# Latent attention: features of queries and keys on the partitions, both latents scaled once, the non-rotary transposes gone

## The chip, the cores and the metric

The kernel runs on one core of one Trainium2 chip. The metric is the device time of one execution, in microseconds. The kernel before took 1671.33 us (median of 3 runs, 1671.21 to 1671.62).

## The reference, cut to what matters

One block of a hybrid encoder, 256 tokens, model width 2048: latent attention with 16 heads, a convolution branch, gates, an attention over a memory, a SwiGLU. The change is in the latent attention alone:

```python
q = (rms_norm(c_q, norm_cq) @ w_uq).reshape(B, S, MLA_HEADS, QK_NOPE + QK_ROPE)      # 512 -> 16 x (128 + 64)
q = jnp.concatenate([q[..., :QK_NOPE], apply_rope(q[..., QK_NOPE:], cos, sin)], axis=-1)
kv = (rms_norm(c_kv, norm_ckv) @ w_ukv).reshape(B, S, MLA_HEADS, QK_NOPE + V_HEAD)   # 256 -> 16 x (128 + 128)
k_nope, v = kv[..., :QK_NOPE], kv[..., QK_NOPE:]
k_r = apply_rope(k_rope[:, :, None, :], cos, sin)                                    # one rotary key for all heads
```

The scores of a head are the product of its query and key over 128 non-rotary and 64 rotary features; a softmax with a chunk-causal mask and the product with v follow.

## The kernel before, in words

All weights stream through a ring of four tiles (128 x 1024 f32 at most). SP issues one DMA a tile into `raw`; ACT rounds the tile to fp32r (`split_hi`, L776 to L782, tile `w_hi`), DVE makes the remainder (`split_lo`, L1254 to L1260, tile `w_lo`), and TensorE (PE) multiplies three times per block of 128 input features: lo by hi, hi by lo, hi by hi (`products`, L349 to L369, the matmuls on L364 to L366). Here the activations are the stationary operand (128 features x 128 tokens) and the weights the moving one (512 columns), so the product comes out with tokens on the partitions, in `acc`, two PSUM banks, one for each half of the tokens. `tile_done` gives a ring slot back to ACT and `acc_free[b]` a bank to PE.

The order is written by hand, for each engine. The parts that the change touches:

- **Projection (L431 to L472).** Tiles 0 to 7 make c_q (512 columns), tiles 8 to 15 c_kv and the rotary key (320 columns); four chunks of eight tiles for the convolution follow. ACT copies c_q and later c_kv to `stage` and sums its squares; POOL makes the row factors 1/rms (`row_factor`, L1849). PE turns c_q's `stage` behind the second of the tiles 8 to 15 (`pos == 1`, L460), c_kv's behind the second tile of the next chunk (L467), the turned rotary key behind the fourth (L470). ACT and DVE turn these into `cqT` and `ckvT` with the gains of the norms (L865, L906, L1327, L1373). The factors 1/rms are not applied yet.
- **Eight pairs of heads (`gate_and_pair`, L528 for PE, L956 for ACT, L1450 for DVE).** A pair is eight gate tiles, two tiles of w_uq (`tile_products`, L564 to L581: 384 moving columns, 24 matmuls), two half-wide tiles of w_ukv (`kv_products`, L548 to L562: 512 columns, 12 matmuls). ACT copies the queries to `q_tok` and keys and values to `kv_tok`, tokens on the partitions, and applies 1/rms there (L970 to L984). POOL turns the rotary queries by their angles (`query_rope`, L1893) into `qr_tok`.
- **Attention of a pair, spread over the gate tiles of the next one (`attention`, L475 for PE, L925 for ACT).** Behind gate tile 1 PE transposes q_tok (4 blocks), kv_tok (4) and qr_tok (2), and ACT copies them to `qnT`, `knT`, `qrT` (features on the partitions). Behind tile 3 come the scores, behind tile 6 the transposes of the probabilities, behind tile 7 the product with the values.

Of the kernel before, what the change touches and what calls it, by code (L numbers as in the profile page):

```python
# [24 lines left out]
ALU = mybir.AluOpType  # L25
# [66 lines left out]
def program(nc, x, memT, positions, vecs, w_in, w_uq, w_ukv, w_dwT, w_pw2, b_pw2, w_o, w_q_mem, w_kv_mem,  # L92
# [10 lines left out]
    with ctx:  # L103
# [54 lines left out]
        q_tok = sb(early, "q_tok", [P, NB, 2, NOPE + ROPE])  # L158
        kv_tok = sb(early, "kv_tok", [P, NB, 2, NOPE + VH])
# [72 lines left out]
        qr_turned, qr_out = sem("qr_turned"), sem("qr_out")  # L232
# [112 lines left out]
        def _(pe):  # L345
# [95 lines left out]
            for t in range(8, 16):  # L441
# [18 lines left out]
                if pos == 1:  # L460
                    turn_stage(Q_CQ, 2 * (S_A + 1))


            for c in range(4):
                for t in range(8):
                    products(T_B + 8 * c, t, 8, mixT, 2 * t, 2, CH, C_B + c)
                    if t == 1 and c == 0:  # L467
                        pe.wait_ge(stage_full, 2 * (S_A + 2))
                        turn_group(Q_CKV, 0, [stage[:, b, k * P:(k + 1) * P] for k in range(2) for b in range(NB)])
                    if t == 3 and c == 0:  # L470
                        pe.wait_ge(kr_ready, 1)
                        turn_group(Q_CKV, 1, [qr_tok[:, b, :, :].rearrange("p h d -> p (h d)") for b in range(NB)])  # L472


            def attention(t, p, q):  # L475

                if t == 0:
                    pe.wait_ge(q_ready, 2 * p + 2)
                    turn_group(q, 0, [q_tok[:, b, h, 0:NOPE] for h in range(2) for b in range(NB)])
                    pe.wait_ge(kv_ready, 2 * p + 2)  # L480
                    turn_group(q, 1, [kv_tok[:, b, h, 0:NOPE] for h in range(2) for b in range(NB)])
                if t == 1:
                    pe.wait_ge(rope_ready, p + 1)
                    if not (isinstance(p, int) and p == 0):
                        pe.wait_ge(qr_out, p)
                    for b in range(NB):
                        ins = turn(xt[:, b * P:(b + 1) * P], qr_tok[:, b, :, :].rearrange("p h d -> p (h d)"),
                                   ident[:, :])
                    ins.then_inc(qr_turned, 1)
                if t == 2:  # L490
                    operand_ready(q)
                    pe.wait_ge(qr_out, p + 1)
# [22 lines left out]
                if t == 7:  # L515
# [3 lines left out]
                    for h in range(2):  # L519
                        mm(ov[:, h * VH:(h + 1) * VH], probsT[:, h, 0:P], kv_tok[:, 0, h, NOPE:],  # L520
                           start=True, stop=True)
                        for kb in range(2):
                            ins = mm(ov[:, (2 + h) * VH:(3 + h) * VH], probsT[:, h, (1 + kb) * P:(2 + kb) * P],  # L523
                                     kv_tok[:, kb, h, NOPE:], start=kb == 0, stop=kb == 1)
# [3 lines left out]
            def gate_and_pair(i, first, last=False):  # L528
# [15 lines left out]
                for t in range(2):  # L544
                    tile_products(i * 12 + T_C, 8 + t, t, 2, cqT, 2 * t, 2, UQ, i * 3 + (C_C + 1))
                kv_products(i * 12 + T_C, i * 3 + (C_C + 2))

            def kv_products(base, chunk):  # L548

                pe.wait_ge(lo_done, base + 12)  # L550
                for b in range(NB):
                    pe.wait_ge(acc_free[b], chunk)
                    for k in range(2):
                        hi, lo = (ckvT[j][:, k, b * P:(b + 1) * P] for j in range(2))
                        whi, wlo = w_hi[:, (10 + k) % RING, 0:CH], w_lo[:, (10 + k) % RING, 0:CH]
                        mm(acc[:, b, :], lo, whi, start=k == 0, stop=False)  # L556
                        mm(acc[:, b, :], hi, wlo, start=False, stop=False)
                        ins = mm(acc[:, b, :], hi, whi, start=False, stop=k == 1)
                        if b == 1:
                            ins.then_inc(tile_done, 1)  # L560
                    if b == 0:
                        ins.then_inc(acc0_full, 1)  # L562

            def tile_products(base, t, pos, n_tiles, lhs, k0, kt, n, chunk):  # L564

                s = t % RING
                first, last = pos == 0, pos == n_tiles - 1
                pe.wait_ge(lo_done, base + (t + 1))
                for b in range(NB):
                    if first:  # L570
                        pe.wait_ge(acc_free[b], chunk)
                    for k in range(kt):
                        hi = lhs[0][:, k0 + k, b * P:(b + 1) * P]
                        lo = lhs[1][:, k0 + k, b * P:(b + 1) * P]
                        o = acc[:, b, 0:n]
                        mm(o, lo, w_hi[:, s, k * n:(k + 1) * n], start=first and k == 0, stop=False)  # L576
                        mm(o, hi, w_lo[:, s, k * n:(k + 1) * n], start=False, stop=False)  # L577
                        ins = mm(o, hi, w_hi[:, s, k * n:(k + 1) * n], start=False, stop=last and k == kt - 1)  # L578
                    if last and b == 0:
                        ins.then_inc(acc0_full, 1)  # L580
# [192 lines left out]
        def _(act):  # L773
# [85 lines left out]
            for t in range(8):  # L859
# [5 lines left out]
                if t == 2:  # L865
# [25 lines left out]
            for c in range(4):  # L891
                for t in range(8):
# [13 lines left out]
                    if c == 0 and t == 2:  # L906
                        turned_hi_part(0, 2 * Q_CKV + 1, [ckvT[0][:, k, :] for k in range(2)],
                                       gain=[vcol("norm_ckv", k) for k in range(2)])
                    if c == 0 and t == 4:
# [15 lines left out]
            def attention(t, p, q):  # L925
                if t == 0:
                    act.wait_ge(turned, 2 * q + 1)
# [5 lines left out]
                if t == 1:  # L933
                    act.wait_ge(qr_turned, p + 1)
                    fn(qrT[:, :], xt[:, 0:TOK], ACT.Copy).then_inc(qr_out, 1)
# [20 lines left out]
            def gate_and_pair(i, first, last=False):  # L956
                for t in range(12):
# [7 lines left out]
                    if t == 9:  # L965

                        if not first:
                            act.wait_ge(turned, 2 * i + (2 * Q_C - 1))
                            act.wait_ge(rope_ready, i)
                        for b in range(NB):  # L970
# [1006 lines left out]
```

## Time and profile before

| | |
|---|---|
| median of 3 runs | 1671.33 us |
| the profiled execution's own time | 1671.39 us |
| its span in the trace | 1669.6 us |
| around the span | 1.8 us |
| PE (matmul) busy | 1653.5 us, 99% |
| PEld (weight load) busy | 1375.3 us, 82% |
| DVE / ACT / POOL busy | 1127.3 / 827.7 / 102.2 us |

A row of the timeline gives the start of an instruction (or of several alike, merged, with their count), its duration and its engine. The matmuls are pipelined and the ends in their rows are modelled: a matmul's duration is longer than the time until the next one starts. What a matmul costs is read from start to start.

### The profile page before, as it was taken

The page shows a single profiled execution, that of the slowest core. Times are in us where ns is not written, and L with a number is a line of the kernel's source. Part 1 is how long each engine was busy: PE and PEld are TensorE (multiplying, and loading weights), DVE is VectorE, ACT ScalarE, POOL GpSimd, SP SyncE. Part 2 cuts the span into 40 slices and gives each one's busy share as a digit, 9 for nine tenths or more (in the row PEclk, how much of TensorE's full clock was granted, in tenths as well). Part 3 has the DMA queues.
Part 4 walks back from the last instruction along what each step waited for, and adds up shares of the span by engine and source line. Part 5 has one row for each costly group of instructions (what it writes and reads, how often), then busy time and mean ns, then how long its engine had stood idle before and what let it go on. Part 6 is the DMA issues. An engine that isn't in the chain of part 4 may idle for free.

```text
span 1669.6 us, 23695 instructions
## 1 busy us (share of the span) xinstructions
PE 1653.5 (99%) x7696; PEld 1375.3 (82%) x7696; DVE 1127.3 (68%) x1461; ACT 827.7 (50%) x1057; POOL 102.2 (6%) x152
## 2 busy tenths in 40 slices
PE   9999999999999999999999999999999999999997
PEld 7888888888888888878888788888888888888886
DVE  5578777778986457886559856666666666654453
ACT  7556555556546444566545644444444444444343
POOL 3100100011000000120001200000000000000000
PEclk9999999999999999999999999999999999999999
DMA  7865555555675665554445666666666666565563
GB/s 228 248 208 163 168 165 154 166 157 165 182 212 181 192 212 182 182 190 158 144 139 187 190 191 198 191 191 196 184 187 198 201 191 198 191 219 184 182 213 134
DMA packets 161106, 309.68 MB, mean 185 GB/s; under 512 B 10240, under 2 KB 16896, under 8 KB 160800
## 3 DMA queue, kind: packets, MB, share of 16 engines
q1 hardware_dynamic: 158864, 301.50, 58.8%
q0 software_dynamic: 1488, 6.42, 1.0%
q10 hardware_dynamic: 704, 1.11, 0.2%
q8 instruction: 29, 0.48, 0.1%
q14 instruction: 21, 0.17, 0.0%
HBM read 306.89 MB, written 2.10 MB: 185 GB/s over the span
## 4 chain that ended last, share of the span: by engine, by line
PE 91%; DVE 4%; issue 2%; ACT 1%; DMA 0%; SPq 0%; DVEq 0%; ACTq 0%; POOLq 0%; POOL 0%
PE acc L364 28%; PE acc L366 27%; PE acc L365 27%; DVE w_lo L1259 2%; PE tp L376 1%; DVE x_f L1598 1%; PE acc L576 1%; PE acc L578 1%; PE acc L577 1%; PE sc L499 1%; DMA raw<-in_w_in_dram 0%; PE ov L523 0%; ACT w_hi L782 0%; PE sc L504 0%; PE acc L556 0%
## 5 line engine op out<-in xcount | busy, mean ns | idle before, releaser
L1259 DVE TENSOR_TENSOR w_lo<-raw,w_hi 128x1024 fp32r<-128x1024 f32 (+3 forms) x591 | 718.0, 1220 | 432.4 <-ACT w_hi L782 422.4
L782 ACT ACTIVATE w_hi<-raw 128x1024 fp32r<-128x1024 f32 (+3 forms) x591 | 605.5, 1027 | 758.6 <-PE acc L366 726.1
L364 PE MATMUL acc<-w_hi,crossT 128*128 128x512 f32 x832 | 324.8, 390 | 0.8 <-DVEq L1616 0.8
L366 PE MATMUL acc<-w_hi,crossT 128*128 128x512 f32 x832 | 323.9, 389 | 0.0
L365 PE MATMUL acc<-w_lo,crossT 128*128 128x512 f32 x832 | 323.8, 389 | 0.0
L364 PE MATMUL acc<-w_hi,mixT 128*128 128x512 f32 x732 | 290.0, 396 | 1.8 <-ACTq L877 0.5
L366 PE MATMUL acc<-w_hi,mixT 128*128 128x512 f32 x732 | 285.6, 390 | 0.0
L365 PE MATMUL acc<-w_lo,mixT 128*128 128x512 f32 x732 | 285.0, 389 | 0.0
L364 PEld LDWEIGHTS acc<-w_hi,crossT 128*128 128x128 f32 x832 | 156.2, 188 | 33.9 <-issue 1.5
L366 PEld LDWEIGHTS acc<-w_hi,crossT 128*128 128x128 f32 x832 | 156.2, 188 | 32.5
L365 PEld LDWEIGHTS acc<-w_lo,crossT 128*128 128x128 f32 x832 | 156.2, 188 | 32.1
L364 PEld LDWEIGHTS acc<-w_hi,mixT 128*128 128x128 f32 x732 | 137.4, 188 | 35.2 <-issue 4.8
L366 PEld LDWEIGHTS acc<-w_hi,mixT 128*128 128x128 f32 x732 | 137.4, 188 | 29.5
L365 PEld LDWEIGHTS acc<-w_lo,mixT 128*128 128x128 f32 x732 | 137.6, 188 | 27.2
L1391 DVE SCALAR_TENSOR_TENSOR conv<-uT,wdwT,conv (+1 forms) x240 | 118.2, 493 | 19.5 <-DVE conv L1391 16.7
L366 PE MATMUL acc<-w_hi,actT 128*128 128x512 f32 x336 | 130.7, 389 | 0.0
L365 PE MATMUL acc<-w_lo,actT 128*128 128x512 f32 x336 | 130.7, 389 | 0.0
L364 PE MATMUL acc<-w_hi,actT 128*128 128x512 f32 x336 | 130.7, 389 | 0.0
L1725 DVE STREAM_TRANSPOSE row_bc<-stage 32x256 f32<-32x256 f32 x176 | 76.7, 436 | 3.6
L364 PEld LDWEIGHTS acc<-w_hi,actT 128*128 128x128 f32 x336 | 63.1, 188 | 13.2
L366 PEld LDWEIGHTS acc<-w_hi,actT 128*128 128x128 f32 x336 | 63.1, 188 | 13.2
L365 PEld LDWEIGHTS acc<-w_lo,actT 128*128 128x128 f32 x336 | 63.1, 188 | 12.8
(264 smaller groups left out, 1527.0 us busy)
## 6 DMA issues: line engine op xcount, KB each, us to landing
raw<-in_w_in_dram SPq DMA_DIRECT2D x104, 512.0 KB, 3.8
raw<-in_w_gate_dram SPq DMA_DIRECT2D x88, 512.0 KB, 4.3
raw<-in_w_up_dram SPq DMA_DIRECT2D x88, 512.0 KB, 3.8
raw<-in_w_down_dram SPq DMA_DIRECT2D x80, 512.0 KB, 4.0
raw<-in_w_kv_mem_dram SPq DMA_DIRECT2D x64, 512.0 KB, 3.9
raw<-in_w_o_dram SPq DMA_DIRECT2D x32, 512.0 KB, 4.4
raw<-in_w_q_mem_dram SPq DMA_DIRECT2D x32, 512.0 KB, 3.7
raw<-in_w_o_mem_dram SPq DMA_DIRECT2D x32, 512.0 KB, 3.7
```

What stands on the lines that cost most here:

```text
L364: mm(o, lo, whi, start=first and k == 0, stop=False)
L365: mm(o, hi, wlo, start=False, stop=False)
L366: ins = mm(o, hi, whi, start=False, stop=end)
L376: ins = turn(tp[:, bank, j * P:(j + 1) * P], src, ident[:, :])
L499: mm(sc[:, h, at:at + keys], qnT[:, h, qs:qs + P], knT[:, h, 0:keys], start=qs == 0, stop=False, skip_group_check=True)
L576: mm(o, lo, w_hi[:, s, k * n:(k + 1) * n], start=first and k == 0, stop=False)
L577: mm(o, hi, w_lo[:, s, k * n:(k + 1) * n], start=False, stop=False)
L578: ins = mm(o, hi, w_hi[:, s, k * n:(k + 1) * n], start=False, stop=last and k == kt - 1)
L782: fn(w_hi[:, s, 0:width], raw[:, s, 0:width], ACT.Copy).then_inc(hi_done, 1)
L1259: V.tensor_tensor(w_lo[:, s, 0:width], raw[:, s, 0:width], w_hi[:, s, 0:width].bitcast(F32), ALU.subtract).then_inc(lo_done, 1)
L1391: ins = V.scalar_tensor_tensor(out=a, in0=u, scalar=wt, in1=a, op0=ALU.mult, op1=ALU.add)
L1725: ins = V.transpose(dst[:, :, :, 32 * i:32 * i + 32], src[:, :, :, 32 * j:32 * j + 32])
```

## The change

The non-rotary queries and the keys are made with the weights stationary (128 input features x 128 output features) and the turned latent moving (256 tokens), so they come out of `acc` with the features on the partitions, and ACT copies them straight to `qnT` and `knT`. The rotary queries and the values are still made with tokens on the partitions, now 128 and 256 moving columns. Since a row factor can't be applied to a token that lies on the columns, POOL scales both latents in `stage` before they are turned, and the turns move to later tiles. Only the rotary queries are still transposed, each half through a bank of `tp`.

In the diff, in the order of the file: PE's projection, attention, `kv_products` and `q_products` (which takes the place of `tile_products`), ACT, DVE, POOL.

```diff
-                if pos == 1:
+                if pos == 5:
+                    pe.wait_ge(cq_scaled, 2)
                     turn_stage(Q_CQ, 2 * (S_A + 1))
...
-                    if t == 1 and c == 0:
-                        pe.wait_ge(stage_full, 2 * (S_A + 2))
+                    if t == 4 and c == 0:
+                        pe.wait_ge(ckv_scaled, 2)
                         turn_group(Q_CKV, 0, [stage[:, b, k * P:(k + 1) * P] for k in range(2) for b in range(NB)])
-                    if t == 3 and c == 0:
                         pe.wait_ge(kr_ready, 1)
                         turn_group(Q_CKV, 1, [qr_tok[:, b, :, :].rearrange("p h d -> p (h d)") for b in range(NB)])
...
-                if t == 0:
-                    pe.wait_ge(q_ready, 2 * p + 2)
-                    turn_group(q, 0, [q_tok[:, b, h, 0:NOPE] for h in range(2) for b in range(NB)])
-                    pe.wait_ge(kv_ready, 2 * p + 2)
-                    turn_group(q, 1, [kv_tok[:, b, h, 0:NOPE] for h in range(2) for b in range(NB)])
...
-                        ins = turn(xt[:, b * P:(b + 1) * P], qr_tok[:, b, :, :].rearrange("p h d -> p (h d)"),
-                                   ident[:, :])
-                    ins.then_inc(qr_turned, 1)
+                        turn_group(q, b, [qr_tok[:, b, :, :].rearrange("p h d -> p (h d)")])
...
+                    pe.wait_ge(q_ready, 2 * p + 2)
+                    pe.wait_ge(kv_ready, 2 * p + 2)
...
             def kv_products(base, chunk):
 
                 pe.wait_ge(lo_done, base + 12)
+                pe.wait_ge(acc_free[0], chunk)
+                for h in range(2):
+                    o = acc[:, 0, h * TOK:(h + 1) * TOK]
+                    at = slice(h * (NOPE + VH), h * (NOPE + VH) + NOPE)
+                    for k in range(2):
+                        hi, lo = (ckvT[j][:, k, :] for j in range(2))
+                        whi, wlo = w_hi[:, (10 + k) % RING, at], w_lo[:, (10 + k) % RING, at]
+                        mm(o, whi, lo, start=k == 0, stop=False)
+                        mm(o, wlo, hi, start=False, stop=False)
+                        ins = mm(o, whi, hi, start=False, stop=k == 1)
+                ins.then_inc(acc0_full, 1)
+                pe.wait_ge(acc_free[1], chunk)
                 for b in range(NB):
-                    pe.wait_ge(acc_free[b], chunk)
+                    o = acc[:, 1, b * 2 * VH:(b + 1) * 2 * VH]
                     for k in range(2):
                         hi, lo = (ckvT[j][:, k, b * P:(b + 1) * P] for j in range(2))
-                        whi, wlo = w_hi[:, (10 + k) % RING, 0:CH], w_lo[:, (10 + k) % RING, 0:CH]
-                        mm(acc[:, b, :], lo, whi, start=k == 0, stop=False)
-                        mm(acc[:, b, :], hi, wlo, start=False, stop=False)
-                        ins = mm(acc[:, b, :], hi, whi, start=False, stop=k == 1)
+                        whi, wlo = (w[:, (10 + k) % RING, 0:CH].rearrange("p (h d) -> p h d", h=2)[:, :, NOPE:]
...
+            def q_products(base, pos, chunk):
+
+                s = (8 + pos) % RING
+                first, last = pos == 0, pos == 1
+                pe.wait_ge(lo_done, base + (9 + pos))
+                if first:
+                    pe.wait_ge(acc_free[0], chunk)
+                wv = [w[:, s, 0:2 * UQ].rearrange("p (k h d) -> p k h d", k=2, h=2) for w in (w_hi, w_lo)]
+                for h in range(2):
+                    o = acc[:, 0, h * TOK:(h + 1) * TOK]
+                    for k in range(2):
+                        hi, lo = (cqT[j][:, 2 * pos + k, :] for j in range(2))
+                        whi, wlo = (w[:, k, h, 0:NOPE] for w in wv)
+                        mm(o, whi, lo, start=first and h == 0 and k == 0, stop=False, skip_group_check=True)
+                        mm(o, wlo, hi, start=False, stop=False, skip_group_check=True)
+                        ins = mm(o, whi, hi, start=False, stop=last and k == 1, skip_group_check=True)
+                if last:
+                    ins.then_inc(acc0_full, 1)
+                if first:
+                    pe.wait_ge(acc_free[1], chunk)
                 for b in range(NB):
-                    if first:
-                        pe.wait_ge(acc_free[b], chunk)
-                    for k in range(kt):
-                        hi = lhs[0][:, k0 + k, b * P:(b + 1) * P]
-                        lo = lhs[1][:, k0 + k, b * P:(b + 1) * P]
-                        o = acc[:, b, 0:n]
-                        mm(o, lo, w_hi[:, s, k * n:(k + 1) * n], start=first and k == 0, stop=False)
-                        mm(o, hi, w_lo[:, s, k * n:(k + 1) * n], start=False, stop=False)
-                        ins = mm(o, hi, w_hi[:, s, k * n:(k + 1) * n], start=False, stop=last and k == kt - 1)
-                    if last and b == 0:
-                        ins.then_inc(acc0_full, 1)
+                    o = acc[:, 1, b * 2 * ROPE:(b + 1) * 2 * ROPE]
+                    for k in range(2):
+                        hi, lo = (cqT[j][:, 2 * pos + k, b * P:(b + 1) * P] for j in range(2))
+                        whi, wlo = (w[:, k, :, NOPE:] for w in wv)
+                        mm(o, lo, whi, start=first and b == 0 and k == 0, stop=False, skip_group_check=True)
+                        mm(o, hi, wlo, start=False, stop=False, skip_group_check=True)
+                        ins = mm(o, hi, whi, start=False, stop=last and k == 1, skip_group_check=True)
                 ins.then_inc(tile_done, 1)
...
-                if t == 2:
+                if t == 6:
...
-                    if c == 0 and t == 2:
+                    if c == 0 and t == 5:
...
-                    if c == 0 and t == 4:
+                    if c == 0 and t == 5:
...
                         act.wait_ge(scores_ready, 2 * p)
-                    fn(qnT[:, :, :].rearrange("p h t -> p (h t)"), tp[:, 0, :], ACT.Copy).then_inc(turned_out[0], 1)
-                    act.wait_ge(turned, 2 * q + 2)
-                    fn(knT[:, :, :].rearrange("p h t -> p (h t)"), tp[:, 1, :], ACT.Copy).then_inc(turned_out[1], 1)
...
-                    fn(qrT[:, :], xt[:, 0:TOK], ACT.Copy).then_inc(qr_out, 1)
+                    for b in range(NB):
+                        fn(qrT[:, b * P:(b + 1) * P], tp[:, b, 0:P], ACT.Copy).then_inc(turned_out[b], 1)
...
+                            act.wait_ge(scores_ready, 2 * i)
...
-                        for b in range(NB):
+                        for b, (dst, width) in enumerate(((qnT[:, :, :].rearrange("p h t -> p (h t)"), CH),
+                                                          (q_tok[:, :, :, :].rearrange("p b h d -> p (b h d)"), TOK))):
                             acc_full(b, i * 3 + (C_C + 1), i * 12 + (T_C + 10))
-                            fn(q_tok[:, b, :, :].rearrange("p h d -> p (h d)"), acc[:, b, 0:UQ], ACT.Copy,
-                               scale=rfac[:, R_CQ, b:b + 1]).then_inc(q_ready, 1)
+                            fn(dst, acc[:, b, 0:width], ACT.Copy).then_inc(q_ready, 1)
                             act.wait_ge(q_ready, 2 * i + (b + 1))
                             act.sem_inc(acc_free[b], 1)
                     if t == 10:
                         if not first:
                             act.wait_ge(pv_done, i)
-                        for b in range(NB):
+                        for b, dst in enumerate((knT[:, :, :].rearrange("p h t -> p (h t)"),
+                                                 v_tok[:, :, :, :].rearrange("p b h d -> p (b h d)"))):
                             acc_full(b, i * 3 + (C_C + 2), i * 12 + (T_C + 12))
-                            fn(kv_tok[:, b, :, :].rearrange("p h d -> p (h d)"), acc[:, b, :], ACT.Copy,
-                               scale=rfac[:, R_CKV, b:b + 1]).then_inc(kv_ready, 1)
+                            fn(dst, acc[:, b, :], ACT.Copy).then_inc(kv_ready, 1)
                             act.wait_ge(kv_ready, 2 * i + (b + 1))
                             act.sem_inc(acc_free[b], 1)
...
-                if t == 10:
+                if t == 14:
...
-                    if c == 0 and t == 2:
+                    if c == 0 and t == 5:
...
             row_factor(R_CQ)
+            gp.wait_ge(r_ready, R_CQ + 1)
+            for b in range(NB):
+                G.tensor_scalar(stage[:, b, :], stage[:, b, :], rfac[:, R_CQ, b:b + 1], None, ALU.mult)\
+                    .then_inc(cq_scaled, 1)
...
             row_factor(R_CKV)
+            gp.wait_ge(r_ready, R_CKV + 1)
+            for b in range(NB):
+                G.tensor_scalar(stage[:, b, 0:KV_LORA], stage[:, b, 0:KV_LORA], rfac[:, R_CKV, b:b + 1], None,
+                                ALU.mult).then_inc(ckv_scaled, 1)
```

ACT's and DVE's parts of `cqT` and `ckvT` move with the turns (ACT from t == 2 to 6 and from 2 to 5, DVE from 10 to 14 and from 2 to 5); ACT's copy of the rotary key moves from t == 4 to 5.

## Rows read from the trace of the kernel before

**Rows 1.** The page: busy shares, granted clock, the chain by engine.

```profile
PE 1653.5 (99%) x7696; PEld 1375.3 (82%) x7696; DVE 1127.3 (68%) x1461; ACT 827.7 (50%) x1057; POOL 102.2 (6%) x152
...
PEclk9999999999999999999999999999999999999999
...
PE 91%; DVE 4%; issue 2%; ACT 1%; DMA 0%; SPq 0%; DVEq 0%; ACTq 0%; POOLq 0%; POOL 0%
```

**Rows 2.** Timeline of PE, the w_uq and w_ukv tiles of one pair.

```profile
196.08 0.61 PE L523 MATMUL ov<-kv_tok,probsT 128*128 128x128 f32 x4
196.44 0.42 PE L576 MATMUL acc<-w_hi,cqT 128*128 128x384 f32 x1
196.70 0.33 PE L577 MATMUL acc<-w_lo,cqT 128*128 128x384 f32 x1
...
200.54 0.34 PE L578 MATMUL acc<-w_hi,cqT 128*128 128x384 f32 x1
200.72 0.40 PE L556 MATMUL acc<-w_hi,ckvT 128*128 128x512 f32 x1
...
203.24 0.39 PE L558 MATMUL acc<-w_hi,ckvT 128*128 128x512 f32 x1
203.46 0.45 PE L364 MATMUL acc<-w_hi,mixT 128*128 128x512 f32 x1
203.75 0.40 PE L365 MATMUL acc<-w_lo,mixT 128*128 128x512 f32 x1
```

**Rows 3.** Timeline of PE, the transposes of one pair.

```profile
208.99 0.60 PE L376 MATMUL tp<-ident,q_tok 128*128 128x128 f32 x4
209.42 0.60 PE L376 MATMUL tp<-ident,kv_tok 128*128 128x128 f32 x4
209.86 0.38 PE L487 MATMUL xt<-ident,qr_tok 128*128 128x128 f32 x2
210.00 0.48 PE L364 MATMUL acc<-w_hi,mixT 128*128 128x512 f32 x1
```

**Rows 4.** Timeline of PE, 24 fp32r matmuls of 256 columns in the memory attention, twice.

```profile
767.29 0.28 PE L674 MATMUL sc<-row_r,memqT 128*128 128x256 f32 x1
...
770.12 0.40 PE L364 MATMUL acc<-w_hi,crossT 128*128 128x512 f32 x1
...
783.03 0.28 PE L697 MATMUL xt<-probs_mT,val_h 128*128 128x256 f32 x1
...
784.47 0.40 PE L364 MATMUL acc<-w_hi,crossT 128*128 128x512 f32 x1
```

**Rows 5.** Timeline of PE and its weight loads, two f32 products of one column.

```profile
155.99 0.64 PEld L537 LDWEIGHTS xt<-ones,sqT 128*128 128x128 f32 x4
156.22 0.50 PE L537 MATMUL xt<-ones,sqT 128*128 128x1 f32 x4
...
156.55 0.19 PEld L364 LDWEIGHTS acc<-w_hi,mixT 128*128 128x128 f32 x1
156.58 0.49 PE L364 MATMUL acc<-w_hi,mixT 128*128 128x512 f32 x1
```

**Rows 6.** Groups by line: ACT's copies out of acc and of the turned tiles.

```profile
L981 ACT ACTIVATE kv_tok<-acc,rfac 128x512 f32<-128x512 f32 x16 | 10.9, 681 | 2.5 <-PE acc L558 2.4
...
L972 ACT ACTIVATE q_tok<-acc,rfac 128x384 f32<-128x384 f32 x16 | 9.3, 583 | 3.6 <-PE acc L578 3.6
...
L935 ACT ACTIVATE qrT<-xt 128x256 f32<-128x256 f32 x8 | 3.1, 386 | 0.0
```

**Rows 7.** Timeline of POOL: the row factors of c_q and c_kv.

```profile
38.60 0.74 POOL L1851 TENSOR_TENSOR rfac<-mean_sq,minus_half 128x2 f32<-128x2 f32 x1 [9.04 <-DVE mean_sq L1294]
...
55.96 0.71 POOL L1851 TENSOR_TENSOR rfac<-mean_sq,minus_half 128x2 f32<-128x2 f32 x1 [1.95 <-DVE mean_sq L1294]
```

**Rows 8.** Groups by line: POOL's nearest operations to the scaling.

```profile
L1918 POOL COPY xs<-stage 128x1024 f32<-128x1024 f32 x2 | 2.1, 1037 | 202.7 <-DVE stage L1613 202.7
...
L1836 POOL TENSOR_SCALAR resid<-resid 128x128 f32<-128x128 f32 x1 | 1.2, 1207 | 0.1
```

**Rows 9.** Timeline of PE, projection: the turn of c_q, seventh tile of the eight, turn of the key.

```profile
38.34 1.03 PE L376 MATMUL tp<-ident,stage 128*128 128x128 f32 x8
39.14 0.39 PE L454 MATMUL acc<-w_hi,mixT 128*128 128x320 f32 x1
...
46.25 0.31 PE L454 MATMUL acc<-w_hi,mixT 128*128 128x320 f32 x1
...
61.86 0.38 PE L376 MATMUL tp<-ident,qr_tok 128*128 128x128 f32 x2
```

More of the change, by code:

```diff
@@ L157, in program @@
         ckvT = [sb(early, f"ckvT{j}", [P, 2, TOK], F32R) for j in range(2)]
-        q_tok = sb(early, "q_tok", [P, NB, 2, NOPE + ROPE])
-        kv_tok = sb(early, "kv_tok", [P, NB, 2, NOPE + VH])
+        q_tok = sb(early, "q_tok", [P, NB, 2, ROPE])
+        v_tok = sb(early, "v_tok", [P, NB, 2, VH])
+        spare = sb(early, "spare", [P, NB, 2, 2 * NOPE])
         qr_tok = sb(early, "qr_tok", [P, NB, 2, ROPE])
@@ L231, in program @@
         rope_step, rope_ready = sem("rope_step"), sem("rope_ready")
-        qr_turned, qr_out = sem("qr_turned"), sem("qr_out")
+        ckv_scaled = sem("ckv_scaled")
+        cq_scaled = sem("cq_scaled")
         scores_ready, scores_read = sem("scores_ready"), sem("scores_read")
@@ L519, in attention @@
                     for h in range(2):
-                        mm(ov[:, h * VH:(h + 1) * VH], probsT[:, h, 0:P], kv_tok[:, 0, h, NOPE:],
+                        mm(ov[:, h * VH:(h + 1) * VH], probsT[:, h, 0:P], v_tok[:, 0, h, :],
                            start=True, stop=True)
@@ L523, in attention @@
                             ins = mm(ov[:, (2 + h) * VH:(3 + h) * VH], probsT[:, h, (1 + kb) * P:(2 + kb) * P],
-                                     kv_tok[:, kb, h, NOPE:], start=kb == 0, stop=kb == 1)
+                                     v_tok[:, kb, h, :], start=kb == 0, stop=kb == 1)
                     ins.then_inc(pv_done, 1)
@@ L544, in gate_and_pair @@
                 for t in range(2):
[L545 removed]
+                    q_products(i * 12 + T_C, t, i * 3 + (C_C + 1))
                 kv_products(i * 12 + T_C, i * 3 + (C_C + 2))
@@ L551, in kv_products @@
+                ins.then_inc(acc0_full, 1)
+                pe.wait_ge(acc_free[1], chunk)
                 for b in range(NB):
-                    pe.wait_ge(acc_free[b], chunk)
+                    o = acc[:, 1, b * 2 * VH:(b + 1) * 2 * VH]
                     for k in range(2):
                         hi, lo = (ckvT[j][:, k, b * P:(b + 1) * P] for j in range(2))
-                        whi, wlo = w_hi[:, (10 + k) % RING, 0:CH], w_lo[:, (10 + k) % RING, 0:CH]
-                        mm(acc[:, b, :], lo, whi, start=k == 0, stop=False)
-                        mm(acc[:, b, :], hi, wlo, start=False, stop=False)
-                        ins = mm(acc[:, b, :], hi, whi, start=False, stop=k == 1)
+                        whi, wlo = (w[:, (10 + k) % RING, 0:CH].rearrange("p (h d) -> p h d", h=2)[:, :, NOPE:]
+                                    for w in (w_hi, w_lo))
+                        mm(o, lo, whi, start=k == 0, stop=False)
+                        mm(o, hi, wlo, start=False, stop=False)
+                        ins = mm(o, hi, whi, start=False, stop=k == 1)
@@ L1895, in query_rope @@
                 if not first:
-                    gp.wait_ge(qr_turned, p)
-                q = [q_tok[:, :, :, NOPE + 32 * k:NOPE + 32 * k + 32] for k in range(2)]
+                    gp.wait_ge(turned, 2 * p + 2 * Q_C)
+                q = [q_tok[:, :, :, 32 * k:32 * k + 32] for k in range(2)]
                 rope(q, [qr_tok[:, :, :, 32 * k:32 * k + 32] for k in range(2)], 2, rope_step, p, None)\
```

16 lines of the change are left out of this document (2 added, 14 removed).

## The prediction

> **What bounds the kernel now.** First the page: PE is busy for 99% of the span, its granted clock is in the top tenth in all 40 slices (the 2.4 GHz level), and the chain that ended last runs through PE for 91% [rows 1]. DVE and ACT have a third and a half of the span free. So a change pays by what it takes off PE's queue or puts on it; work on ACT, DVE or POOL counts only where PE waits for it. Second, the timeline of PE within a pair: it shows what each shape costs from start to start, since the durations of pipelined matmuls overlap. The pair's attention comes eight times, and in none of its stretches is PE idle before the parts that change.
>
> **What PE pays now, per pair.** The 24 matmuls of 384 columns and the 12 of 512 run from 196.44 to 203.46, 7.02 us [rows 2]. In them are 0.09 us of lead behind the f32 products (the first step is 0.26 us, the later ones 0.17: (200.72 - 196.70) / 23 = 0.175), and the 12 take (203.46 - 200.72) / 12 = 0.228 each. The first matmul behind them needs 0.29 us to its next where 0.23 is usual: 0.06 us, which I take for the wait on the bank that ACT empties. The eight transposes of q_tok and kv_tok take 209.86 - 208.99 = 0.87 us, 0.109 each [rows 3]. Together 7.02 + 0.06 + 0.87 = 7.95 us.
>
> **What takes its place.** Counted in columns nothing is saved: 24 x 384 + 12 x 512 = 15,360 before, and 48 x 256 + 24 x 128 = 15,360 after. But 36 matmuls become 72, each with a weight load of 128 x 128. So the price of a narrow matmul decides.
> - 256 columns, fp32r (24 for the queries' non-rotary part, 12 for the keys, 12 for the values): (770.12 - 767.29) / 24 = 0.118 us in one place and (784.47 - 783.03) / 12 = 0.120 in the other [rows 4]. I take 0.119: 48 x 0.119 = 5.71 us.
> - 128 columns, fp32r (24, the rotary queries): no row shows one. Below: the straight line through the wider ones, (0.228 - 0.119) / 256 columns = 0.00043 us a column, gives 0.119 - 128 x 0.00043 = 0.065. Above: a matmul of 256 columns, 0.119, if width stops to matter; and further off, what an f32 product of 128 columns costs, two recorded matmuls each: four records of L523 start at 196.08, and the next block really starts at 196.44 + 0.09, so 0.11 a record and 0.22 a product [rows 2]. Nearest is the load: the four matmuls of ONE column each (two f32 products, two records each) still take from 156.22 to 156.58, and behind the first of the loads, which is ahead of its matmul, they follow at 0.11 us up to the next at 156.55 [rows 5]. The moving work there is nearly nothing, so 0.11 us is what a weight load of this shape costs when it follows another. Transposes of 128 columns give 0.109 again [rows 3]. I take 0.110: 24 x 0.110 = 2.64 us.
>
> The Trainium skill ("TensorE: Matmul & The Clock Gate", the part on LDWEIGHTS) prices a load by its columns over 1.2 GHz, 107 ns for 128; by that rule, the rows at one column agree. The same page (the part on the issue gap) gives about 81 ns for a sustained matmul of 128 columns, and 131 ns for one of 512; no row here bears out the latter, the same shape takes 0.228 us. The sum by 81 ns is a rival below.
>
> So PE pays 0.09 + 5.71 + 2.64 = 8.44 us a pair if no wait remains: 0.49 us more than 7.95. Eight pairs: +3.9 us. The two transposes of the rotary queries stay and cost the same.
>
> **Waits inside the pair.** The keys' first matmul waits for bank 0, which ACT copies to qnT while PE runs the 12 narrow matmuls of the same tile: 12 x 0.110 = 1.32 us, plus 0.12 for the last wide one, 1.44 us from the last wide start. ACT needs 0.28 us until that matmul ends [rows 4], about 0.14 to start, 0.68 for a 512-wide copy [rows 6], and about 0.12 for its own wait and release: 1.22 us. Hidden, with 0.2 us to spare. If a narrow matmul took under 0.09 us it would not be. Bank 1 (256 wide, 0.39 us by the 256-wide copy in [rows 6], before 0.58) has 12 x 0.119 = 1.43 us, hidden. The next gate chunk waits for knT's bank for as long again, and ACT is now free sooner, so I count the 0.06 us as gone; at worst it stays, +0.5 us in all. ACT loses two 512-wide copies a pair behind gate tile 1; nothing queued behind them is late, so that is worth nothing. The scores wait for two 128-wide copies in place of three wider ones, two gate tiles (5.4 us) earlier: hidden. ACT's qnT now waits for the scores of the pair before, behind gate tile 3, over 10 us earlier: no wait. POOL's rotary work is unchanged, and PE transposes its result some 8 us behind the queries: hidden. The ring slots of the query tiles come back when half of the block is done, as before; those of the two key tiles some 0.3 us later at most, and their next tile is needed two tiles (5.5 us) on.
>
> **The projection.** POOL scales c_q after 38.60 + 0.74 = 39.34 us [rows 7], in two operations of 128 x 512. Its price isn't in the trace. From below: half of a copy of 128 x 1024, 0.52 us; from above: four times the two-step operation on 128 x 128, 4.8 us [rows 8]. PE needs it behind the sixth tile: 46.25 less the 0.80 + 0.08 us of the turn that no longer comes ahead of it [rows 9], 45.4 us. At 0.52 to 2.9 us each it is hidden. c_kv: from 56.67 us on [rows 7], two of 128 x 256, 0.26 to 2.4 us each, so by 61.5 at the latest, and PE asks for it behind the next tile after the old turn of the key, 61.86 - 0.5 + 2.73 = 64.1 us [rows 9]. Hidden. Queued behind the scaling on POOL are the first memory load, needed some 80 us later, and the key's rotation, which waits for c_kv anyway. ACT's and DVE's latent parts move by four and three tiles, and the pairs that use them begin some 90 us later. I count all of this at nothing; if the upper bounds held it would cost what rival 3 says.
>
> **Sum.** The profiled execution took 1671.39 us (its span and 1.8 us around it), 0.06 over the median. 1671.4 + 3.9 = 1675.3 us, +0.23%. About 0.2% (3.3 us) is what a measurement of this kernel can tell from no change, so this lies just beyond it. With both ends of the two prices (0.118 and the 0.1075 of q_tok's four transposes in [rows 3]; 0.120 and 0.119) a pair costs 0.38 to 0.76 us more, +3.0 to +6.1 us; with the 0.06 us kept, up to +6.5.
>
> **The rivals.**
> 1. *Loads don't gate: the price follows the columns, 0.065 us for 128.* Then 24 cost 1.56 us. For: fp32r at 256, 384 and 512 columns lies on one line, with no sign of a floor. Against: the one-column rows. But now bank 0 is late: PE would be at the keys 0.12 + 0.78 = 0.90 us behind the last wide start, ACT at 1.22: 0.32 us of new wait. 0.09 + 5.71 + 1.56 + 0.32 = 7.68, 0.27 less a pair, -2.2 us: 1669.2. Without the wait -4.7 us, 1666.7. This is the side that isn't slower; it decides below about 0.090 us a narrow matmul, where the sum breaks even. Chance 0.13, half of it beyond 0.2%.
> 2. *A narrow fp32r matmul runs at f32's price, 0.22 us.* Nothing narrower than 256 fp32r columns runs in the trace, so a lower rate there can't be excluded; against it, the weight loads of both types last the same 0.19 us. 24 x (0.22 - 0.11) = 2.64 us a pair more: 3.9 + 21.1 = +25.0 us, 1696.4. Chance 0.09.
> 3. *POOL late.* At 4.8 us an operation c_q is scaled at 49.1 us, PE stands from 45.4: +3.7 us, once, on top of the sum: 1679.0. It decides from 2.9 us an operation. Chance 0.03.
> 4. *A stretch of narrow fp32r matmuls hides part of each load.* Midway between the column line and the load, at 0.0875 us, it is 24 x 0.0875 = 2.10 and 0.05 us of wait at bank 0: nothing gained or lost, 1671.4. Chance 0.04. The 81 ns of the Trainium skill's page named above would be near this case (an estimate: 0.7 us faster than now).
>
> That the change doesn't do what it says I leave out: the diff takes out the eight transposes and doubles the matmuls, and both will be counted. A fall of the clock to 1.2 GHz in the narrow stretches has nothing for it: the transposes and one-column products leave the granted clock in the top tenth.
>
> **How the numbers follow.** The forecast's chance is 0.71; its own range is 1674.4 to 1677.9, 0.52 above 0.2% and 0.19 within. Slower: 0.52 + 0.09 + 0.03 = 0.64. Within: 0.19 + 0.07 + 0.04 = 0.30. Faster: 0.06. The range 1669.0 to 1678.0 holds the forecast, rival 4 and the better part of rival 1.
>
> **What would show it.** After: 24 matmuls of 128 columns with starts 0.11 us apart, 48 of 256 at 0.12; 8.4 us from the first query matmul to the next gate tile; no idle time of PE at the keys' first matmul; a period of the pairs 0.5 us longer than now; POOL done with c_q by 45 us, PE not idle ahead of the turn. I am wrong if the narrow matmuls stand 0.07 or 0.2 us apart, or if PE waits at a bank or in the projection.

## The result and the profile after

The changed kernel takes 1677.45 us (median of 7 runs, 1676.62 to 1678.84) against 1671.49 us before: 5.96 us more, a ratio of 1.0036 with a 95% interval of 1.0027 to 1.0045. Slower was forecast, with 1675.3 us as the likeliest time and 1678.0 as the upper end. The direction and the main mechanism held; about a third of the loss came from a place that the prediction had put down at nothing. The profiled execution is the slowest of the seven (1678.84 us), 7.4 us longer than the profiled one of the kernel before, so its rows show more of that loss than the median has.

The page of the changed kernel, to be held against [rows 1]:

```profile
PE 1660.0 (99%) x7920; PEld 1387.6 (83%) x7920; DVE 1126.1 (67%) x1461; ACT 818.0 (49%) x1049; POOL 105.8 (6%) x156
...
PE 92%; DVE 4%; issue 2%; ACT 1%; DMA 0%; DVEq 0%; POOL 0%; ACTq 0%; POOLq 0%; SPq 0%
```

PE has 224 matmuls more: 8 x 36 added, 8 x 8 transposes gone. Its timeline within a pair, the queries first (the first is a wide product behind the f32 ones, and 12 wide, 12 narrow, 12 wide, 12 narrow follow one another; then keys and values):

```profile
200.36 0.36 PE L582 MATMUL acc<-cqT,w_hi 128*128 128x256 f32 x1
...
201.88 0.22 PE L594 MATMUL acc<-w_hi,cqT 128*128 128x128 f32 x1
201.94 0.28 PE L595 MATMUL acc<-w_lo,cqT 128*128 128x128 f32 x1
...
203.06 0.28 PE L596 MATMUL acc<-w_hi,cqT 128*128 128x128 f32 x1
...
205.84 0.28 PE L596 MATMUL acc<-w_hi,cqT 128*128 128x128 f32 x1
205.95 0.33 PE L552 MATMUL acc<-ckvT,w_hi 128*128 128x256 f32 x1
206.12 0.28 PE L553 MATMUL acc<-ckvT,w_lo 128*128 128x256 f32 x1
...
208.76 0.28 PE L565 MATMUL acc<-w_hi,ckvT 128*128 128x256 f32 x1
208.88 0.40 PE L366 MATMUL acc<-w_hi,mixT 128*128 128x512 f32 x1
209.11 0.40 PE L367 MATMUL acc<-w_lo,mixT 128*128 128x512 f32 x1
```

Here a wide matmul is one of 256 moving columns and a narrow one of 128. From start to start a wide one takes (208.76 - 206.12) / 22 = 0.120 us, a narrow one (203.06 - 201.94) / 10 = 0.112. The whole stretch is 208.88 - 200.36 = 8.52 us where 8.44 was forecast and 7.02 + 0.06 + 0.87 = 7.95 stood before [rows 2, 3]: +0.57. The gate matmul behind it has its usual 0.23 us to the next: the 0.06 us of wait has gone, as forecast. The starts of the scores in the chain of waits (`sc`, eight matmuls a pair) give the period of the pairs, of the changed kernel:

```profile
185.28 1.31 PE sc L493 x8
220.22 1.31 PE sc L493 x8
...
394.81 1.31 PE sc L493 x8
430.31 1.31 PE sc L493 x8
```

and of the kernel before:

```profile
181.36 1.31 PE sc L499 x8
215.71 1.31 PE sc L499 x8
...
387.56 1.31 PE sc L499 x8
422.88 1.31 PE sc L499 x8
```

The eight starts have seven steps between them. Six take 34.91 to 34.94 us in place of 34.34 to 34.42, on average 34.92 in place of 34.37: +0.56. The last grows by 0.18 only (35.50 against 35.32). There, ACT also rounds the memory's operands, and before the change PE stood 0.58 us behind the values for the bank; now it is 0.21. With the first pair, which lies ahead of the first scores, the pairs cost about 7 x 0.56 + 0.18 = 4.1 us. But the first scores already start 3.92 us late, of which one pair's share explains 0.56. The other 3.36 us are in the projection, in this execution; of the median's 5.96 us, 5.96 - 4.1 = 1.9 are. The rows of POOL, ACT and PE there, which answer to [rows 7, 9], and between them the landing of one weight tile from the chain of waits (in brackets: idle time before, and who ended it):

```profile
38.50 0.74 POOL L1863 TENSOR_TENSOR rfac<-mean_sq,minus_half 128x2 f32<-128x2 f32 x1 [9.05 <-DVE mean_sq L1306]
39.34 3.14 POOL L1883 TENSOR_SCALAR stage<-stage,rfac 128x512 f32<-128x512 f32 x2
42.42 0.62 POOL L1890 DMA_DIRECT2D xs<-in_memT_dram  x1
...
42.44 7.91 DMA raw<-in_w_in_dram
...
46.71 1.06 ACT L798 ACTIVATE w_hi<-raw 128x1024 fp32r<-128x1024 f32 x1 [1.86 <-DMA raw<-in_w_in_dram]
47.67 1.56 ACT L815 ACTIVATE cqT<-tp,vecT 128x256 fp32r<-128x256 f32 x4
50.37 1.06 ACT L798 ACTIVATE w_hi<-raw 128x1024 fp32r<-128x1024 f32 x1 [1.14 <-DMA raw<-in_w_in_dram]
51.34 0.51 ACT L889 ACTIVATE stage<-acc,rfac 128x320 f32<-128x320 f32 x1
...
52.49 0.76 PE L366 MATMUL acc<-w_hi,mixT 128*128 128x512 f32 x1 [2.65 <-ACTq L893]
53.05 0.63 PE L367 MATMUL acc<-w_lo,mixT 128*128 128x512 f32 x1
53.48 0.63 PE L368 MATMUL acc<-w_hi,mixT 128*128 128x512 f32 x1
```

and in the kernel before:

```profile
39.30 0.58 POOL L1874 DMA_DIRECT2D xs<-in_memT_dram  x1
...
48.27 1.06 ACT L782 ACTIVATE w_hi<-raw 128x1024 fp32r<-128x1024 f32 x1 [0.52 <-PE acc L456]
...
50.39 0.47 PE L364 MATMUL acc<-w_hi,mixT 128*128 128x512 f32 x1 [0.46 <-ACTq L877]
```

POOL's scaling is done by 42.5 us and nobody waits for it. But PE stands 2.65 us in place of 0.46 for a bank that ACT empties; ACT does that behind weight tile 18 in its order, the `w_hi` row at 50.37, and that tile lands about 2 us later than it did. POOL issues the first load of the memory at 42.42 in place of 39.30 (512 KB, not the 1 MB of an expectation below), and tile 18's transfer, issued at 42.44 beside it, takes 7.91 us. The load itself takes 8.1 us to land in place of 5.4. Tile 17, the `w_hi` row at 46.71, is no later than it was (46.69). So PE restarts 52.49 - 50.39 = 2.10 us late. Behind the wait its matmuls are (53.48 - 53.05) = 0.43 us apart, nearly twice the usual 0.23. The clock shows it; the stretch from 50 to 58 us (busy time of each engine, then the granted clock) of the changed kernel, and of the kernel before:

```profile
50.00:58.00 8.00, 5.51 (x18) 4.49 (x19) 4.08 (x6) 5.03 (x9) 2.92 (x7) 0.79 0.68 210
```

```profile
50.00:58.00 8.00, 7.61 (x35) 6.32 (x36) 3.88 (x5) 4.36 (x8) 3.64 (x8) 1.00 0.82 238
```

A mean of 0.79 means that for part of the stretch the clock was at its lower level, 1.2 GHz; before the fall PE had done nothing for 2.65 us. The first seven steps behind the wait take 3.02 us, where the execution of the queries' half below, which kept its clock, takes 1.70: the fall costs 1.3 us. The late restart and the fall, 2.1 + 1.3, make up the 3.4 us of this execution.

### The profile page after: what moved, and what is told of

It reads as the page before. It is cut to its first block, busy times and chain, and to the rows that moved or that the text cites. A ratio compares the mean times of both kernels' runs of the same rounds, so it can differ in the third digit from the quotient of the medians.

```text
span 1677.0 us, 24117 instructions
## 1 busy us (share of the span) xinstructions
PE 1660.0 (99%) x7920; PEld 1387.6 (83%) x7920; DVE 1126.1 (67%) x1461; ACT 818.0 (49%) x1049; POOL 105.8 (6%) x156
## 4 chain that ended last, share of the span: by engine, by line
PE 92%; DVE 4%; issue 2%; ACT 1%; DMA 0%; DVEq 0%; POOL 0%; ACTq 0%; POOLq 0%; SPq 0%
PE acc L366 27%; PE acc L368 27%; PE acc L367 27%; DVE w_lo L1271 2%; DVE x_f L1610 1%; PE tp L378 1%; PE sc L493 1%; PE acc L582 0%; DMA raw<-in_w_in_dram 0%; PE acc L584 0%; PE acc L583 0%; PE acc L595 0%; PE ov L517 0%; PE acc L596 0%; PE sc L498 0%
```

## The experiments

Nine kernels, each timed against the kernel before (medians; its own were 1671.4 to 1671.5).

### Is it the load that prices a narrow matmul?

`e6_narrow64`, from the changed kernel:

```diff
-                    o = acc[:, 1, b * 2 * ROPE:(b + 1) * 2 * ROPE]
+                    o = acc[:, 1, b * 2 * ROPE:b * 2 * ROPE + ROPE]
-                        whi, wlo = (w[:, k, :, NOPE:] for w in wv)
+                        whi, wlo = (w[:, k, 0, NOPE:] for w in wv)
```

> The changed kernel, with the rotary queries' 24 matmuls a pair of 64 columns instead of 128: the second head's rotary queries aren't computed (its columns hold what the bank held before). Theory A (the weight load gates a narrow matmul): the starts stay 0.11 us apart, the time stays at 1677.4 within 0.3. Theory B (columns count, plus a fixed price): 64 columns less are 0.027 us each, 192 of them 5.1 us, 1672.3.

So this kernel leaves out the rotary queries of every second head. Measured: 1677.39 us (1676.87 to 1679.18), ratio 1.0037 [1.0023, 1.0050], the changed kernel's time. Its narrow matmuls on PE's timeline, and two of its loads (PEld):

```profile
202.07 0.20 PE L594 MATMUL acc<-w_hi,cqT 128*128 128x64 f32 x1
202.10 0.28 PE L595 MATMUL acc<-w_lo,cqT 128*128 128x64 f32 x1
202.21 0.28 PE L596 MATMUL acc<-w_hi,cqT 128*128 128x64 f32 x1
...
203.22 0.28 PE L596 MATMUL acc<-w_hi,cqT 128*128 128x64 f32 x1
...
202.07 0.19 PEld L595 LDWEIGHTS acc<-w_lo,cqT 128*128 128x128 f32 x1
202.19 0.19 PEld L596 LDWEIGHTS acc<-w_hi,cqT 128*128 128x128 f32 x1
```

(203.22 - 202.10) / 10 = 0.112 us with half the columns. The period is 34.89 to 34.93 us. Columns are free here. A floor under any matmul, whatever its load, would give the same price, but the first two narrow matmuls stand only 0.03 us apart (202.07 to 202.10; in the changed kernel 0.06, 201.88 to 201.94), so matmuls can start closer than 0.11. What keeps the rest 0.11 us apart is the pace of the 128 x 128 loads, whose rows start 0.11 to 0.12 us apart. Theory B, which would have given 5.1 us, falls, and with it the first rival.

### Which half of the change costs?

`e5_keys_only`, from the kernel before (its main lines; the values' product and ACT's copies as in the change):

```diff
-                    turn_group(q, 1, [kv_tok[:, b, h, 0:NOPE] for h in range(2) for b in range(NB)])
...
+                    turn_group(q, 1, [qr_tok[:, b, :, :].rearrange("p h d -> p (h d)") for b in range(NB)])
...
+                for h in range(2):
+                    o = acc[:, 0, h * TOK:(h + 1) * TOK]
+                    at = slice(h * (NOPE + VH), h * (NOPE + VH) + NOPE)
...
+                        for b, dst in enumerate((knT[:, :, :].rearrange("p h t -> p (h t)"),
+                                                 v_tok[:, :, :, :].rearrange("p b h d -> p (b h d)"))):
```

> Keys and values as in the changed kernel (weights stationary for the keys, 24 matmuls of 256 columns, no transposes of the keys), queries as in the kernel before (24 matmuls of 384, four transposes), c_kv scaled by POOL, c_q not, its turn at the old place. By the prices of the traces: 24 x 0.120 = 2.88 us a pair in place of 12 x 0.228 + 0.06 + 4 x 0.109 = 3.24: -0.36 us a pair, -2.9 us, 1668.6, the pairs' period 34.0 us. Rival: narrower matmuls cost the same 0.5 us wherever they are put, and the keys' part is neutral or slower, 1671.5 to 1673.

Measured: 1668.04 us (1667.58 to 1668.34, 11 runs), ratio 0.9980 [0.9971, 0.9989]: 3.4 us faster than the kernel before, and 9.4 faster than the change. Its scores:

```profile
181.26 1.31 PE sc L493 x8
215.25 1.31 PE sc L493 x8
```

A period of 33.98 to 34.00, 0.38 us less than before (0.36 worked out). The last step gives another 0.15.

`e7_queries_only`, from the changed kernel:

```diff
+                if t == 0:
+                    pe.wait_ge(kv_ready, 2 * p + 2)
+                    turn_group(q, 0, [kv_tok[:, b, h, 0:NOPE] for h in range(2) for b in range(NB)])
...
+                    for k in range(2):
+                        hi, lo = (ckvT[j][:, k, b * P:(b + 1) * P] for j in range(2))
+                        whi, wlo = w_hi[:, (10 + k) % RING, 0:CH], w_lo[:, (10 + k) % RING, 0:CH]
```

> The complement: queries as in the changed kernel (24 matmuls of 256 and 24 of 128 a pair), keys and values as in the kernel before (12 of 512 and four transposes), both latents scaled as in the changed kernel. By the prices of the traces the queries' part costs 24 x 0.120 + 24 x 0.1115 = 5.56 us in place of 24 x 0.1745 + 4 x 0.109 = 4.62: +0.93 us a pair, +7.4, and the projection's wait 2.0 on top: 1681, with a period of the pairs of 35.3 us. If the keys' part gains nothing, it is 1677.5.

Measured: 1681.30 us (1679.64 to 1681.63), ratio 1.0059 [1.0045, 1.0073], a period of 35.21 to 35.22 us: +0.85 a pair (0.93 expected, see the next experiment for the difference). So the keys' half gains and the queries' half loses more than twice as much. The reason is in the shapes: the keys trade 12 matmuls of 512 columns and four transposes for 24 of 256, none of them narrow; the queries trade 24 of 384 and four transposes for 24 of 256 and 24 of 128, and 24 x 0.112 = 2.7 us is paid for columns that 24 x 128 x 0.00043 = 1.3 us would cover (a column: the 0.23 us of 512 less the 0.120 of 256, by 256).

### What happened in the projection?

`e4_prologue_only`, from the kernel before:

```diff
-                if pos == 1:
+                if pos == 5:
+                    pe.wait_ge(cq_scaled, 2)
...
-                               scale=rfac[:, R_CQ, b:b + 1]).then_inc(q_ready, 1)
+                               scale=1.0).then_inc(q_ready, 1)
```

> The kernel before with the projection's part of the change alone: POOL scales both latents in stage, the turns and ACT's and DVE's parts of them move to the later tiles, ACT's copies out of acc in the pairs scale by 1.0. The pairs' matmuls and transposes are those of the kernel before. If the projection's new wait and the pairs' matmuls are the two terms and add up, this is about 2.0 us over the kernel before, 1673.5, with the pairs' period at 34.35 us. If the 0.5 us a pair came from anything other than the matmuls and transposes (the copies' scale, the latents), the period would move here too.

Measured: 1674.31 us (1672.62 to 1674.78, 11 runs), ratio 1.0015 [1.0006, 1.0024]: +2.8 where 2.0 was expected. PE's wait is there, 2.65 us, with a mean clock of 0.79 in the profiled execution. So the projection's cost exists without the pairs' matmuls, and the pairs' 0.56 us don't come from the copies' scale. The period is 34.28 to 34.32, 0.07 less than before, because the wait behind the keys and values has gone:

```profile
206.96 0.39 PE L366 MATMUL acc<-w_hi,mixT 128*128 128x512 f32 x1
207.18 0.39 PE L367 MATMUL acc<-w_lo,mixT 128*128 128x512 f32 x1
```

The pairs of this kernel differ from those before only in ACT's copies, which no longer apply a row factor: kv_tok's takes 0.59 us in place of 0.68 [rows 6]. So the 0.06 us are won by the cheaper copy and not by the new matmuls. Against this kernel, whose latents and copies are the same, the queries' half costs 35.22 - 34.30 = 0.92 us a pair, the 0.93 expected, and the keys' half then takes 35.22 - 34.92 = 0.30 off.

`e1_mem_first`, from the changed kernel:

```diff
             row_factor(R_CQ)
-            gp.wait_ge(r_ready, R_CQ + 1)
-            for b in range(NB):
-                G.tensor_scalar(stage[:, b, :], stage[:, b, :], rfac[:, R_CQ, b:b + 1], None, ALU.mult)\
-                    .then_inc(cq_scaled, 1)
...
             load_memory(0)
+            gp.wait_ge(r_ready, R_CQ + 1)
+            for b in range(NB):
+                G.tensor_scalar(stage[:, b, :], stage[:, b, :], rfac[:, R_CQ, b:b + 1], None, ALU.mult)\
+                    .then_inc(cq_scaled, 1)
```

> The changed kernel with one difference: POOL issues the first load of the memory before it scales c_q (as in the kernel before), not behind it. In the changed kernel that 1 MB load starts at 42.4 us in place of 39.3, tile 18 of the weights lands 2 us later (ACT starts on it at 50.37 instead of 48.27), ACT empties PE's bank only behind it, and PE stands 2.65 us. Theory A (the load's place in time delays the weights): tile 18 is back by 48.5, ACT goes cqT, tile 18, stage; PE restarts by 51.5 instead of 52.5, 1 to 2 us of the changed kernel's time come back: about 1676.0. Theory B (ACT's c_q part ahead of that copy is what delays): the wait stays at 2.6 us, time as the changed kernel, 1677.4.

`e2_act_late`, from the changed kernel (DVE's part in the same way):

```diff
-                if t == 6:
-                    for g in range(2):
-                        turned_hi_part(g, 2 * Q_CQ + g + 1, [cqT[0][:, 2 * g + k, :] for k in range(2)],
...
+                    if c == 0 and t == 1:
+                        for g in range(2):
+                            turned_hi_part(g, 2 * Q_CQ + g + 1, [cqT[0][:, 2 * g + k, :] for k in range(2)],
```

> The changed kernel with ACT's and DVE's part of the turned c_q (1.6 us on each) moved from the last tiles of the projection to behind the second tile of the next chunk, POOL's order left. Theory A (late weights): ACT still stands for tile 18 until about 50.4, nothing comes back, 1677.4. Theory B (ACT's order): the bank is free by about 50.6, PE stands about 0.6 us, 2 us come back, 1675.5.

`e3_both` has the two edits together.

> Both edits together: the first load of the memory ahead of the scaling, and ACT's and DVE's c_q part behind the second tile of the next chunk. Both theories: PE restarts at about 50.4 as in the kernel before, the granted clock doesn't fall there, and only the pairs' 0.50 us x 8 = 4.0 us are left over the kernel before: 1675.5 (+0.24%). If more than 4.5 us are left, the pairs cost more than their period shows.

Measured: the load first 1675.98 us (1675.81 to 1676.33), ratio 1.0027 [1.0017, 1.0038]; ACT late 1678.95 us (1676.57 to 1679.59), 1.0039 [1.0025, 1.0053]; both 1675.10 us (1674.86 to 1676.65), 1.0023 [1.0014, 1.0032]. The load first:

```profile
39.39 0.58 POOL L1886 DMA_DIRECT2D xs<-in_memT_dram  x1
...
49.23 1.07 ACT L798 ACTIVATE w_hi<-raw 128x1024 fp32r<-128x1024 f32 x1
...
51.37 0.47 PE L366 MATMUL acc<-w_hi,mixT 128*128 128x512 f32 x1 [1.33 <-ACTq L893]
```

ACT late:

```profile
50.57 1.06 ACT L798 ACTIVATE w_hi<-raw 128x1024 fp32r<-128x1024 f32 x1 [3.63 <-DMA raw<-in_w_in_dram]
...
52.69 0.47 PE L366 MATMUL acc<-w_hi,mixT 128*128 128x512 f32 x1 [2.70 <-ACTq L889]
```

Both:

```profile
50.29 0.47 PE L366 MATMUL acc<-w_hi,mixT 128*128 128x512 f32 x1 [0.46 <-ACTq L889]
```

Theory A, that the load's place in time delays the weights, is shown, and theory B, ACT's order alone, is refuted. With the load back in its place tile 18 is there when ACT comes to it (no idle time before 49.23), and PE's wait halves, to 1.33 us. Moving ACT's 1.56 us of work alone gives nothing: ACT only stands the longer for the tile, 3.63 us. (Its median lies 1.5 us above the changed kernel's and above the 1677.4 of theory A, but the two spreads overlap; the next experiment bears on them.) Yet the second edit isn't idle: behind the first it takes the rest of the wait, 1.33 to 0.46 us. It was the second limit in the row, hidden by the late tile. With both, 3.6 us are left over the kernel before (4.0 between the two profiled executions, 4.1 by the periods).

`e9_kept_busy`, from the changed kernel:

```diff
+            keep_busy(11)
```

> The changed kernel with PE kept at work in the projection's new wait: 11 f32 products of the identity with itself, 128 columns each, written to a bank that nothing reads, between the last projection tile and the next chunk. They fill about 2.4 of the 2.65 us. Theory A (in some executions the granted clock falls in that wait, and the first matmuls behind it run at half speed; this makes the changed kernel's runs spread from 1676.6 to 1678.8): no fall, all runs within 0.7 us of each other at about 1676.7. Theory B (the spread comes from the weights' landing times): the runs spread over 2 us as before, median 1677.4.

Measured: 1677.57 us, 1677.12 to 1677.74 in 5 runs, ratio 1.0035 [1.0022, 1.0049]. The clock stayed up (mean 1.00 from 50 to 58 us) and PE went on at 52.63 us with 0.23 us between matmuls:

```profile
50.15 2.62 PE L396 MATMUL ov<-ident 128*128 128x128 f32 x22
52.63 0.47 PE L366 MATMUL acc<-w_hi,mixT 128*128 128x512 f32 x1
52.94 0.40 PE L367 MATMUL acc<-w_lo,mixT 128*128 128x512 f32 x1
```

In the profiled execution PE restarts later than in the changed kernel's (52.63 against 52.49), and yet the first scores start at 184.08 in place of 185.28, and its whole time is 1.27 us shorter: that is what the fall cost there. Over all runs it is half a hit: the spread shrank from 2.2 to 0.6 us and the runs above 1678 are gone, which fits a clock that falls in some executions. It isn't shown run by run, since only one execution of each kernel was profiled, and five runs are few. (The five runs with ACT late lie at 1676.6, 1676.8 and then 1679.0 to 1679.6, with nothing between; one profiled execution, of the queries alone, waited 2.75 us and kept its clock.) But the median did not come down to 1676.7: it lies where the changed kernel's profiled execution would lie without its fall (1678.84 - 1.3 = 1677.5), and above that kernel's three lowest runs (1676.62 to 1677.04). Whether the filling, which ends about when the bank is freed, or the weights' landing in these five runs cost that, wasn't tried.

### Does ACT's copy bound PE once the narrow matmuls get fewer?

`e8_two_products`, from the kernel with both edits:

```diff
                         mm(o, lo, whi, start=first and b == 0 and k == 0, stop=False, skip_group_check=True)
-                        mm(o, hi, wlo, start=False, stop=False, skip_group_check=True)
```

> The kernel of the run before with both edits of the projection (1675.1), with two of the three products in the rotary queries: hi by lo of the weights is left out, so 16 narrow matmuls a pair in place of 24. At 0.111 us each this takes 0.89 us a pair off PE. Theory A (ACT's copy of the queries' bank takes 1.2 us from the last wide matmul's start, as the prediction worked out, and PE now arrives at 0.12 + 8 x 0.111 = 1.01): 0.2 us of new wait at the keys' first matmul, 0.68 us a pair, -5.4 us, 1669.7. Theory B (no wait there): -7.1 us, 1668.0.

Measured: 1668.82 us (1668.57 to 1669.36, 11 runs), ratio 0.9984 [0.9975, 0.9993]: 6.3 us less than with both edits, between the two theories. (It is faster than the kernel before only because it leaves a product out.) The bank's wait is there, but smaller:

```profile
200.42 0.28 PE L595 MATMUL acc<-w_hi,cqT 128*128 128x128 f32 x1
200.58 0.39 PE L552 MATMUL acc<-ckvT,w_hi 128*128 128x256 f32 x1
200.81 0.28 PE L553 MATMUL acc<-ckvT,w_lo 128*128 128x256 f32 x1
```

0.39 us from the last narrow matmul to the second wide one, where the change shows 0.28 (205.84 to 206.12): 0.11 us of wait instead of 0.2. 8 x (0.89 - 0.11) = 6.2 us. ACT's 512-wide copy without a row factor takes 0.60 us, not the 0.68 of kv_tok in [rows 6].

## Why the prediction was right, and where it wasn't

- **What bounds it, and the price by start to start**: right. PE's queue is the bound in the pairs, and equal columns don't mean equal time.
- **256 columns**: 0.119 taken, 0.120 measured. **128 columns**: 0.110 taken, 0.112 measured, and 0.112 at 64 columns. The choice of the load as the nearest row [rows 5] was the step that decided the sign, and it was sound. The rival by columns, f32's price, and the partly hidden load are all excluded. A term that it didn't name, a floor under any matmul, is excluded by the two starts 0.03 us apart. The load's 107 ns by the Trainium skill ("TensorE: Matmul & The Clock Gate", the part on LDWEIGHTS) lies 5% under the measured 0.112; the same page's 81 ns for a sustained matmul of 128 columns isn't borne out here.
- **A pair**: 0.49 us more expected, 0.57 measured in the stretch and 0.56 in six of the seven steps between scores. The two prices make the 0.08 of difference. The seventh step, 0.18, had an ACT wait of its own that is shorter now; the prediction looked only at a middle pair.
- **Waits in the pair**: right, none at the keys' bank, and the 0.06 us went. But it priced ACT's copies at their old 0.68 us; without the row factor they take 0.59, and that alone takes the wait away, as `e4_prologue_only` shows. Its 1.22 us for ACT's way to the bank was about 0.1 too long (the copy: 0.60 for 0.68).
- **The projection at nothing**: the step that failed. The prediction priced POOL's scaling well enough (1.58 us an operation, within 0.52 to 4.8) and asked who waits for its result. About the memory load queued behind it, it said only that it is "needed some 80 us later". It didn't ask what a transfer of 512 KB collides with when it starts 3.1 us later: weight tile 18, issued in the same 0.1 us, which ACT must take before it frees PE's bank. The DMA engines' busy share from 46 to 50 us was 0.95, where it had been 0.84, and tile 18 took 7.91 us. It also put ACT's c_q part at nothing by asking when c_q is needed, not what stands behind the part in ACT's own order: the copy that frees the bank. Together some 2 us in the median, and the fall of the clock, 1.3 us, in some executions. Its rival 3 had PE wait in the projection too, but for POOL's result, and no engine waited for that.
- **The sum**: 1675.3 forecast; the kernel with the projection mended takes 1675.10. What was missing was in the main that one term; that the two agree to 0.2 us is partly luck, since the periods make the pairs' part 4.1 us and not 3.9.
- **The range**: 1677.45 lies under its upper end of 1678.0 by luck. The room above 1675.3 was reckoned for dearer narrow matmuls, and the projection's wait filled it; two of the seven runs lie above 1678.0.

## What to carry to other kernels

Price a matmul by columns only above the width at which they cover its weight load; here 256 columns take 0.120 us, and 128 and 64 both 0.112. Turning an operand's layout in the product pays for a transpose where the new shapes stay wide (keys: -0.38 us a pair) and not where it leaves a narrow remainder (queries: +0.85), so try the halves apart: the keys alone beat both kernels, at 1668.04 us. And when work is put ahead of a DMA on a queue, ask not only when its data is needed but which other transfers it will now meet.

## What the runs showed of the hardware that wasn't expected

- Half the columns, the same time: fp32r matmuls of 128 and of 64 moving columns, each with its own 128 x 128 load, both start 0.112 us apart; yet the first two of a stretch start 0.06 and 0.03 us apart.
- After 2.65 to 2.75 us without work PE's granted clock fell to 1.2 GHz in four profiled executions and in a fifth it didn't. In two of the four the very first matmuls behind the wait were slow (0.43 us between 512-column ones in place of 0.23), in the other two only those from about the fourth on. After 1.33 us it hadn't fallen in the profiled one, and those runs spread over 0.5 us only.
- Two transfers of 512 KB issued at 42.42 and 42.44 us took 8.1 and 7.91 us to land; where the first was issued at 39.3 or 39.4 us, it took 5.4 and 5.2.
- ACT's copy of 128 x 512 f32 out of PSUM takes 0.68 us with a scale by partition and 0.59 to 0.60 with none.
- POOL's scaling of 128 x 512 f32 by a per-partition factor took 1.58 us, and of 128 x 256 1.27 us: a fifth less for half the work.
